# Decode attention over a paged latent cache: units of 16 pages, turned by DVE in 32x32 squares, scores on sixteen tiles, two fetch queues

## What is computed

```python
# per sample n, 16 heads; l = 8192 past tokens
q_lat  = einsum('nthd,chd->nthc', q_nope, w_uk)                  # 256 values a head
s_past = (einsum('nthc,nlc->nhtl', q_lat, past_ckv)
          + einsum('nthr,nlr->nhtl', q_rope, past_kr)) * MLA_SCALE
s_new  = ...                                                     # the token itself
p      = softmax(concatenate([s_past, s_new], -1))
o_lat  = einsum('nhtl,nlc->nthc', p[..., :l], past_ckv) + ...    # 256 values a head
o      = einsum('nthc,chd->nthd', o_lat, w_uv)
```

## Time and profile before

| | us |
|---|---|
| median of 3 runs | 3492.07 (3490.07 to 3496.64) |
| the profiled execution | 3496.9 |
| its span, first to last instruction | 3494.7 |
| PE busy (weight loads apart) | 3119.3, 89% |
| DVE busy | 1784.7, 51% |
| ACT busy | 693.3, 20% |
| POOL busy | 878.2, 25% |
| mean granted clock of PE | 0.953 |

### The profile page before, as it was taken

One profiled execution on the slowest core, in us unless ns is written; L12 is line 12 of the kernel. 1 busy time (PEld: TensorE's weight loads), 2 busy tenths in 40 slices (PEclk: granted clock), 3 DMA queues, 4 the chain that ended last, 5 costly groups with the idle time before them and its releaser, 6 DMA issues. The chain is left out here.

```text
span 3494.7 us, 58782 instructions
## 1 busy us (share of the span) xinstructions
PE 3119.3 (89%) x21927; PEld 2794.6 (80%) x21927; DVE 1784.7 (51%) x2928; ACT 693.3 (20%) x1443; POOL 878.2 (25%) x496
## 2 busy tenths in 40 slices
PE   7736788888888888899999999999879999999996
PEld 7623465666676666899999999999549999999996
DVE  4288264554645555365244343566774643525254
ACT  2010132333323332121000000110551210000001
POOL 3100000000001110444343434442004444344332
PEclk9867899999989998999999999999989999999998
DMA  2000100010056664211111111120211111111112
GB/s 99 12 14 15 42 12 13 0 37 0 0 161 195 195 194 122 97 57 47 44 48 44 49 40 55 39 67 25 80 55 51 55 39 51 44 53 41 49 41 70
DMA packets 129070, 205.44 MB, mean 59 GB/s; under 512 B 14817, under 2 KB 95713, under 8 KB 128258
## 3 DMA queue, kind: packets, MB, share of 16 engines
q1 hardware_dynamic: 127810, 199.81, 18.9%
q10 hardware_dynamic: 1152, 4.23, 0.3%
HBM read 189.61 MB, written 6.25 MB: 56 GB/s over the span
## 5 line engine op out<-in xcount | busy, mean ns | idle before, releaser
L136 PE MATMUL ps_trunk_out<-sb_h_hi,sb_slab_hi 128*128 128x344 f32 x2400 | 768.0, 320 | 0.0
L137 PE MATMUL ps_trunk_out<-sb_h_hi,sb_slab_lo 128*128 128x344 f32 x2400 | 764.8, 319 | 0.0
L138 PE MATMUL ps_trunk_out<-sb_h_lo,sb_slab_hi 128*128 128x344 f32 x2400 | 764.4, 319 | 0.0
L120 POOL TENSOR_TENSOR sb_slab_hi<-sb_slab_raw,sb_ones 128x1024 fp32r<-128x1024 f32 (+3 forms) x214 | 345.7, 1616 | 1361.2 <-PE ps_trunk_out L138 1051.6
L122 POOL TENSOR_TENSOR sb_slab_lo<-sb_slab_raw,sb_slab_hi 128x1024 fp32r<-128x1024 f32 (+3 forms) x214 | 485.7, 2270 | 16.8
L137 PEld LDWEIGHTS ps_trunk_out<-sb_h_hi,sb_slab_lo 128*128 128x128 f32 x2400 | 450.4, 188 | 0.6
L136 PEld LDWEIGHTS ps_trunk_out<-sb_h_hi,sb_slab_hi 128*128 128x128 f32 x2400 | 450.3, 188 | 0.6
L138 PEld LDWEIGHTS ps_trunk_out<-sb_h_lo,sb_slab_hi 128*128 128x128 f32 x2400 | 450.4, 188 | 0.0
L1314 POOL TENSOR_TENSOR sb_dec_kr<-sb_dec_ck,sb_ones 128x256 f32<-128x256 f32 x64 | 46.7, 729 | 1199.4 <-DMA sb_dec_ck<-cache 1103.1
L136 PE MATMUL ps_trunk_out<-sb_ffn_a_hi,sb_slab_hi 128*128 128x344 f32 x1056 | 336.9, 319 | 4.9 <-DVEq L1586 4.9
L138 PE MATMUL ps_trunk_out<-sb_ffn_a_lo,sb_slab_hi 128*128 128x344 f32 x1056 | 337.9, 320 | 0.0
(11 more groups left out here) (386 smaller groups left out, 5163.2 us busy)
## 6 DMA issues: line engine op xcount, KB each, us to landing
sb_dec_ck<-cache SPq DMA_DIRECT2D x512, 144.0 KB, 2.4
sb_slab_raw<-f_w_gu SPq DMA_DIRECT2D x88, 512.0 KB, 3.5
sb_slab_raw<-f_w_down SPq DMA_DIRECT2D x32, 384.0 KB, 3.1
sb_slab_raw<-f_w_down SPq DMA_DIRECT2D x32, 320.0 KB, 2.9
sb_slab_raw<-e_w_out SPq DMA_DIRECT2D x24, 256.0 KB, 2.6
sb_slab_raw<-o_w_in SPq DMA_DIRECT2D x12, 512.0 KB, 3.4
sb_slab_raw<-e_w_in SPq DMA_DIRECT2D x10, 512.0 KB, 3.3
sb_x_first<-x SPq DMA_DIRECT2D x8, 516.0 KB, 8.4
```

Of the source, the lines that this page charges most:

```text
L120: nc.gpsimd.tensor_tensor(hi, raw, one, ALU.mult).then_inc(self.hi_done[s], 1)
L136: nc.tensor.matmul(out[:, t, 0:TT], a, x_hi(k)[:, cols], start=k == 0, stop=False)
L137: nc.tensor.matmul(out[:, t, 0:TT], b, x_hi(k)[:, cols], start=False, stop=False)
L138: last = nc.tensor.matmul(out[:, t, 0:TT], a, x_lo(k)[:, cols], start=False, stop=k == kc - 1)
```

## The change

The stage is written anew, and nothing outside it is touched.

- **Units.** The work goes in 32 units of 16 pages, four to a sample, all written out; there is no loop. Three slots of `ck` hold a unit each.
- **Fetch.** A page goes to 32 partitions, four neighbouring tokens (4 x 288 values) to a partition. Pages 4g to 4g+3 of a unit form group g, and page q of a group lies on partitions 32q to 32q+31. SP fetches groups 0 to 2, ACT group 3. The DMA of unit w waits for the values of unit w-3.
- **Turn.** DVE transposes `ck` in 32x32 squares from SBUF to SBUF (`ckT`), one instruction of 128x1152 values for each group. PE's transposes of the pages, POOL's gather and the copies from PSUM are gone.
- **Scores.** The 288 values of a token are 9 blocks of 32. Each matmul multiplies 32 rows by 32 columns and streams 128 values; for each of the 9 blocks there are 16 of them, one for each pair of row group b and column group g, into partitions of g and bank b. The rope part is the ninth block.
- **Softmax and values.** As before, but over 512 columns at a time; 4 transposes of probabilities and 16 matmuls of values a unit. `prob`, `probT` and `o_all` lie in parts of `z` that are free.
- **Queries.** `qall` is set up once, by DVE and ACT.

```diff
+            def fetch(eng, kind, w, g):
+                if w >= CKS:
+                    eng.wait_ge(pv_done, w - CKS + 1)
+                _, numbers = nc.values_load_multi_w_load_instructions(
...
+                for q, page in enumerate(numbers):
+                    eng.dma_start(ck[32 * q:32 * q + 32, w % CKS, g * GP:(g + 1) * GP, :],
+                                  A["cache"][bass.ds(page, 1)].rearrange("a (p s) c -> p (a s) c", s=4)
+                                  ).then_inc(page_in[(w % CKS) * 4 + g], 16)
...
                 def _(sp):
...
-                    with sp.Fori(0, NS) as n:
-                        for c in range(NCH):
-                            sp.wait_ge(pv_done, n * NCH + (c + 1))
...
+                    for w in range(WU):
+                        for g in range(3):
+                            fetch(sp, mybir.EngineType.SP, w, g)
...
                 def _(pe):
...
+                    def scores(w):
+                        if w % NU == 0:
+                            pe.wait_ge(q_ready, w // NU + 1)
+                        pe.wait_ge(turned, w + 1)
+                        if w:
+                            pe.wait_ge(p_done, w)
+                        x = w % 2
+                        for j in range(NJ):
+                            for g in range(4):
+                                for b in range(4):
+                                    m = MM(bank[quads[g], b, 0:P], qc[quads[b], (w // NU) % 2, j, :],
+                                           ckT[quads[b], x, g * GP:(g + 1) * GP, 32 * j:32 * j + 32],
+                                           start=j == 0, stop=j == NJ - 1)
+                        m.then_inc(s_done, 1)
...
+                    def weighted(w):
+                        x = w % 2
+                        pe.wait_ge(p_done, w + 1)
+                        if w >= 2:
+                            pe.wait_ge(pt_ev, w - 1)
+                        for q in range(GP):
+                            m = nc.tensor.transpose(bank[:, 4 + x, q * P:(q + 1) * P], prob[:, x, q, :], ident[:, :])
+                        m.then_inc(pt_done, 1)
...
+                        pe.wait_ge(pt_ev, w + 1)
+                        if w >= 2:
+                            pe.wait_ge(o_ev, w - 1)
+                        for q in range(GP):
+                            for g in range(4):
+                                m = MM(bank[quads[g], 6 + x, 0:KVL], probT[:, x, q, quads[g]],
+                                       ck[:, w % CKS, g * GP + q, 0:KVL], start=q == 0, stop=q == GP - 1)
                         m.then_inc(pv_done, 1)
...
+                    scores(0)
+                    for w in range(1, WU):
+                        scores(w)
+                        weighted(w - 1)
+                    weighted(WU - 1)
...
-                @block.gpsimd
-                def _(pool):
...
                 def _(act):
...
+                    for w in range(WU):
+                        x, k = w % 2, slice(w % 2, w % 2 + 1)
+                        act.wait_ge(mx_done, w + 1)
...
                         nc.scalar.activation(decay[:, k], drop[:, k], ACT.Exp, scale=MLA_SCALE).then_inc(p_done, 1)
...
+                        act.wait_ge(pt_done, w + 1)
+                        if w >= 2:
+                            act.wait_ge(pv_done, w - 1)
+                        nc.scalar.copy(probT[:, x].rearrange("p a t -> p (a t)"), bank[:, 4 + x, :]).then_inc(pt_ev, 1)
+                        if w >= 1 and w + CKS - 1 < WU:
+                            fetch(act, mybir.EngineType.Activation, w + CKS - 1, 3)
...
                 def _(dve):
...
+                    def turn(w, groups):
+                        for g in groups:
+                            dve.wait_ge(page_in[(w % CKS) * 4 + g], (w // CKS + 1) * 16 * GP)
+                            m = V.transpose(ckT[:, w % 2, g * GP:(g + 1) * GP, :].rearrange("p a c -> p (a c)"),
+                                            ck[:, w % CKS, g * GP:(g + 1) * GP, :].rearrange("p a c -> p (a c)"))
+                        if 3 in groups:
+                            m.then_inc(turned, 1)
...
+                    turn(0, (0, 1, 2, 3))
+                    queries(0)
+                    for w in range(WU):
+                        if w + 1 < WU:
+                            turn(w + 1, (0, 1))
+                        maximum(w)
+                        if w % NU == NU - 1 and w + 1 < WU:
+                            queries(w // NU + 1)
+                        if w + 1 < WU:
+                            turn(w + 1, (2, 3))
+                        if w:
+                            outputs(w - 1)
+                    outputs(WU - 1)
```

More of the change, by code:

```diff
@@ L1268, in sample @@
-                    def sample(n, before):
-                        for c in range(NCH):
-                            prev = previous(n, c, before)
-                            turn(n, c, None)
-                            turn(n, c, 0)
-                            if prev:
-                                turn_probs(*prev)
-                            turn(n, c, 1)
-                            scores(n, c, 0)
-                            if prev:
-                                values(*prev)
-                            scores(n, c, 1)
@@ L1316, in read_out @@
-                def read_out(eng, copy, n, parity, c, q, sem_ev):
-                    for half in range(1 if q is None else 2):
-                        b = index((c, q, half))
-                        if b % 2 != parity:
-                            continue
-                        eng.wait_ge(t_done, n * NB + (b + 1))
-                        eng.wait_ge(s_done, n * NCH * NQ + (c * NQ + (4 if q is None else q + 3)))
-                        dst = kT[:, :, :] if q is None else cT[:, q, half, :, :]
-                        copy(dst, bank[:, b % 4, 0:(NQ if q is None else 4) * P].rearrange("p (a b) -> p a b", b=P)).then_inc(sem_ev, 1)
+                by_block = lambda ap: ap.rearrange("p n (a j) h -> p a n j h", a=2)
@@ L1359, in _ @@
-                    act.wait_ge(dve_i, 2)
-                    sample(0, None)
-                    with act.Fori(0, NS - 1) as n:
-                        sample(n + 1, n)
-                    exponential(NS - 1, NCH - 1)
-                    turned_probs(NS - 1, NCH - 1)
+                    act.wait_ge(pages_in, 16)
+                    for w in range(CKS):
+                        fetch(act, mybir.EngineType.Activation, w, 3)
+                    act.wait_ge(dve_i, 1)
+                    for b in range(2, 4):
+                        for j in range(4):
+                            m = nc.scalar.copy(by_block(qall[quads[b]])[:, :, :, j, :], ql[quads[j]])
@@ L1385, in _ @@
                     dve.sem_inc(dve_i, 1)
+                    for b in range(2):
+                        for j in range(4):
+                            m = V.tensor_copy(by_block(qall[quads[b]])[:, :, :, j, :], ql[quads[j]])
+                    ch.mark(m)
                     dve.wait_ge(pe_i, 2)
@@ L1421, in sample @@
-                    def sample(n, before):
-                        for c in range(NCH):
-                            prev = previous(n, c, before)
-                            if prev:
-                                maximum(*prev)
-                            if c == 0:
-                                queries(n)
-                            for q in (None, 0, 1):
-                                read_out(dve, V.tensor_copy, n, 1, c, q, td_ev)
-                            if prev:
-                                outputs(*prev)
```

194 lines of the change are left out of this document (47 added, 147 removed).

## The result

| | before | changed |
|---|---|---|
| median of the runs, us | 3491.07 (4 runs, 3489.93 to 3496.64) | **3570.76** (4 runs, 3566.77 to 3576.46) |
| ratio, 95% interval | | **1.0229** (1.0217 to 1.0242) |
| decode loop, us | 389.4 | 464.8, first turn at 998.0 to the last values' end at 1462.8 |
| period of 16 pages, us | 12.17 | 14.6 |

The change makes the kernel slower by 80 us; the forecast was 44 us faster. In every table here a unit's **block** runs from its first score matmul to the end of its last, its **gaps** are the holes inside the block, and the **stretch** goes from there to the next unit's first score matmul; all are read unit by unit from the timeline of PE, as means over the last 30 of the 32 units (the first two run without values between them).

What follows compares the result with a forecast made beforehand. ACT's late page fetch was taken as the new bound: scores 3.7 plus 6.9 us give a 10.6 us period, 31 of them plus both ends 344 us against 389.4. Forecast 3447 us (-45), its own range 3416 to 3472, overall 3380 to 3560.

Steps and rivals of the forecast that it cites:

- S: PE's score matmuls of one unit: 288 records 13 ns apart, 3.7 us, with bounds of 2.0 and 8.2 us.
- The clock: PE's granted clock, not in the sum: a third of the time at 1.2 GHz, up to 0.2 us a unit, 6 us.
- anything else: Catch-all rival, such as a mix ending near zero or loading PE's written-out code; chance 0.04.
- Head and tail: Loop's ends: turns and queries 5.9 us, then first scores; behind, maximum 1.7, exponential 0.9, transposes 0.7, copy 0.6, values 2.0.
- The stretch of 6.9 us: From scores' end to the next scores: transposes, page numbers, ACT's late fetch of group 3, landing 2.4, turn 1.4; 6.9 us.
- scores held up by starting: Rival on PE's scores: records start no faster than 28.6 ns, S = 8.2, +99 us, 3591 us; chance 0.16.
- The transfers: Page DMA: 2.36 MB, 223 GB/s; landing of 4 us and more, with SP's groups late too, would show the forecast wrong.
- The turn: DVE's 32x32 transpose of a group: one pass, 1.35 us; the rival of two passes gave +21 us, 3513, chance 0.05.

Runs made afterwards that it cites:

- e7: Changed kernel with two page buffers, ACT's fetch ahead of its transpose wait, one more transpose a unit, PE looping over two units: 3910.29 us, ratio 1.1187.
- e16: Changed kernel with all pages on SP's queue and 72 score matmuls of 256 columns for 144 of 128, half the scores left out: 3499.68 us.
- e4: Changed kernel with four more 128x128x512 matmuls behind each unit's values, to hold the clock: 3593.48 us, ratio 1.0295.
- e5: Changed kernel with no page transfers after the first three units, whose pages are turned and scored again: 3455.06 us (one run).
- e1: Changed kernel with ACT's fetch of group 3 moved ahead of its wait for the probability transposes: 3618.31 us, ratio 1.0365.
- e15: As e14, but all pages fetched by SP's queue: 3478.64 us, ratio 0.9958 against the kernel before.
- e12: Changed kernel with one turned-page buffer, scores in two halves of eight tiles, three page buffers, PE looping over three units: 3543.26 us, ratio 1.0145.
- e14: As e13, but with PE's code written out instead of looped: 3512.90 us, ratio 1.0063.
- e2: Changed kernel with 64 columns instead of 128 in each score matmul from unit 1 on, half the scores left out: 3578.62 us (one run).
- e13: As e12, but four page buffers, two of exponentials, turned exponentials and values, and PE looping over four units: 3539.22 us, ratio 1.0127.
- e9 to e11: Changed kernel with PE looping over six units: otherwise unchanged, with ACT's fetch ahead, or with all pages on SP: 3563.37, 3609.91 and 3545.83 us.

## Why the prediction was wrong

By its own steps:
- **The score block is the term that failed: S = 3.7 us forecast, 7.3 found.** The excess of 3.6 a unit and 0.4 more in the stretch are 4.0 x 31 = 124 us, as much as lies between 3447 and 3571; the loop with its turns took 465 us and not 344. The rate behind it was right at full clock (288 x 12.8 ns = 3.7), but three things lie on top. Gaps for code loading take 1.6, shown by e7 and e16 and by the landing of the packets. The clock takes 1.0 to 1.2: 63% of the records are 19.5 ns apart and not 13.1, which is 1.0, and e4 got 1.2 back at 0.89. The rest, about 0.9, is the time in which a record runs out with none behind it, 0.26 to 0.41 us each: once at the end of the block, which 288 x 13 ns left out, and once before each gap (38 in 30 units), which the sum of the gaps leaves out. That is why e5, at a clock of 0.96, still takes 4.4 us without its gaps and not 3.7.
- **The clock**, "up to 0.2 us a unit, 6 us", was too small by a factor of five or six. The prediction took a third of the time at the lower level and let only part of that touch the scores; but PE idles for 5.4 of the 14.6 us of each period, 63% of the score records ran at the lower level, and they were then 19.5 ns apart, not 13.8. The prediction's own PE share of 60% came out as 63% (287 of 453).
- **The written-out code** was in the text as "anything else" with others, at 0.04 together. That was the cause of about half the miss (1.6 us of gaps and 0.5 of records that run out before them, of 4.0; e16 got back 2.2). It could have been priced from what stood there: 648 instructions a unit instead of 288 for 16 pages, none of them run twice, in bursts of 576 within 3.7 us, against a loop whose code was fetched once. The trace before had ten code packets, some 10 us apart, without a hole in the scores; none of its rows showed PE at such a pace through new code, so the bounds of this term had to be far apart.
- **Head and tail** held: from the first turn to the first score matmul 5.5 us (5.9 forecast), from the last scores to the end of the last values 6.4 (5.9). The stage began 6.7 us later than before (970.7 against 964.0 us), but this differs from execution to execution (960 to 971 in the runs here) and is not the change's.
- **The stretch of 6.9 us** held (7.3): four issues by ACT 1.75 us (1.8 forecast), landing 2.8 to 3.0 (2.4), turn 1.37 (1.35), DVE waiting for DMA ahead of it. e1 shows that this bound couldn't simply be lifted: with ACT's fetch moved forward, pages landed in 5.2 us and the gaps doubled.
- **The rival "scores held up by starting"** gave 3591 us, near the time found, and by the wrong mechanism: it had starts 28.6 ns apart, and they are 12.8 at full clock. That its number is near is luck. The rule in the Trainium skill ("TensorE: Matmul & The Clock Gate", Wait — 56ns, not 53.3ns?) of no start under about 25 ns does not hold for these rows on sixteen tiles at full clock.
- **The transfers** were no bound in the changed kernel: 155 GB/s, while e15 moves 193 into the same 32-partition squares. The turn was one pass.

The Trainium skill ("Runtime: NRT & Kernel Launch", Instruction fetch mechanics) says that PE's instruction memory is refilled in blocks of 256 instructions, 16 KiB, in sequence, and that this is hidden behind the pace at which instructions are dispatched. The trace agrees on the blocks (16.4 KB a packet, holes 128 records apart) and disagrees on hidden: 1.6 us of a unit in the changed kernel, 3.5 in e1. The same section of the Trainium skill gives PE room for 2,048 instructions. Here a loop of 1,310 stayed (e7) and one of 1,960, though under that figure, did not (e12).

What stays open: why code packets start later when both queues have pages in flight (e1); why gaps are longer in e14 than in the changed kernel, and why e15, which asks for its code sooner, has fewer; how far between 1,310 and 1,960 a loop may grow; and what e16's matmuls would give in a complete kernel, where half the partitions would hold the scores and maximum and exponential have twice the elements. No run shows it.

## What to carry to other kernels

When a change writes a loop out or trades few large instructions for many small ones, count PE's instructions (weight loads too) per microsecond of its bursts, and look at the packets of the instruction queue: 576 instructions wanted in 3.7 us brought 41 holes at the some 72 places where a block of scores passes from one 256 to the next, and 288 in the same work brought none. Prefer fewer, longer matmuls, or a loop short enough to stay. And where a change leaves PE idle for a third of each period, as here (37%, clock 0.73), price its next burst at the lower level too, and ask of a late transfer that is moved forward what it will then collide with.

## What the runs showed of the hardware

- Sixteen 32x32 tiles start fp32 records of 128 columns 12.8 to 13.1 ns apart at full clock, and 19.5 ns at the lower level; with 64 columns 9.9 and 13.2 (e2). 256-column records on eight tiles take 4.12 us for 144, 26 ns apart, 209 ns a tile.
- A hole for code took 0.3 to 2.4 us in the changed kernel, up to 2.1 with no pages in flight (e5), and up to 4.6 with both queues' (e1). It ended 1.2 to 1.7 us after a 16 KB packet had landed. In the changed kernel's loop no two packets started less than 3.6 us apart, and in no written-out kernel less than 3.2.
- A 32x32 turn of 128x1152 fp32 values on DVE takes 1374 ns, 1.2 ns a value and partition, from SBUF to SBUF.
- A loop of 1,310 PE instructions was fetched once (e7); one of 1,960 was loaded again on each pass (e12). Against writing it out that was 26 us slower (e13 against e14), or 7 to 13 us faster (e9 to e11, on other chips than their twins).
